# The low half of the attention key, stacked twice: a two-layer decoder trunk on one core

## The chip, the core and the metric

The program runs on one core of one Trainium2 chip. The core has a matrix engine (TensorE, "PE" in the profile, with its weight loads shown apart as "PEld"), a vector engine (VectorE, DVE), an activation engine (ScalarE, ACT), GpSimd (POOL) and a queue engine that issues the DMAs (SyncE, SP). They run side by side and wait for each other by semaphores. TensorE's clock has two levels, 1.2 and 2.4 GHz; the profile gives the granted clock as a share of the full one (0.50 and 1.00). The metric is the device time of the whole program in microseconds; lower is better.

## The reference

The input is one sequence of 1024 positions by 1024 channels in float32. Layer 0 projects it to queries (8 heads of 64), one key and one value of 64 that all heads share, an indexer, and two gating halves. Attention takes for every query the 256 best causal keys by the indexer's score:

```
score = where(causal, einsum(w_idx, relu(qi @ ki.T)), -inf)
idx   = top_k(score, 256)
att   = (q . k[idx]) * 64 ** -0.5          # 8 heads, shared k
out   = softmax(att) @ v[idx]
```

q and k are RMS-normed and rotated. The gating branch and attention are concatenated and projected, and the input is added. An MLP (hidden 4096, squared ReLU), a Conformer convolution module (width 31) and a second MLP follow, each with a residual.

## The kernel before

Every float32 product that matters is made from rounded parts ("fp32r"). A value x is split into hi, which is x rounded to fp32r, and lo = x - hi. The large products add hi*hi, hi*lo and lo*hi (L450 to L452, `products`), each with 128 contraction rows.

In attention the head size is only 64, so the parts are stacked along the contraction rows instead. `q_stack` holds a query head's [hi, lo]; transposed, `q_t` has q_hi in rows 0 to 63 and q_lo in rows 64 to 127. `k_t` holds k_hi twice, in rows 0 to 63 and 64 to 127. One product of 128 rows, L594, so gives (q_hi + q_lo) * k_hi. A second product of 64 rows, L595, adds q_hi * k_lo: it takes rows 0 to 63 of `q_t` and `k_lo_t`, which has 64 rows. Both accumulate in the same PSUM bank:

```
nc.tensor.matmul(dst, q_t[t % 2][:, h, :], k_t[:, c0:c1], start=True, stop=False)
mm = nc.tensor.matmul(dst, q_t[t % 2][0:HD, h, :], k_lo_t[:, c0:c1], start=False, stop=t >= 2)
```

Here HD is 64, P is 128, and t is the query tile of 128 positions, h the head. Tile t sees 128(t+1) keys, in pieces of up to 512 columns and at least 256, so that a head has one pair of products in tiles 0 to 3 and two pairs in tiles 4 to 7. That makes 96 products on either line. In tiles 0 and 1 a product with the triangle (L598) adds the causal mask.

The keys are made during the projections, one tile of 128 positions at a time (`process_keys`, VectorE): after norm and rotation, `k_stack[:, 0:2]` gets k twice, rounded, and `k_stack[:, 2]` gets k minus the rounded part (L1340). `turn_keys` (TensorE, L476 by way of `transpose_group`) transposes the first two, then the third (to 64 rows of PSUM), then the indexer's key. `keys_out` (ScalarE, L969 to L971) copies the results to `k_t`, `k_lo_t` and `ki_t`.

Attention runs in two halves, `attention(0)` for query tiles 0 to 3 and `attention(1)` for tiles 4 to 7; between them lie the first output projection and the MLP of the first half, beside which VectorE does the top-k of tiles 4 to 7. Within a half, heads are numbered a = 8t + h, and the order on TensorE is written out in the loop over a: scores(a), turn_probs(a-2), values(a-3). `scores` waits until VectorE has masked head a-2, whose two PSUM banks it takes over. VectorE adds the mask of the chosen keys and takes the row's maximum (L1490; in tiles 0 and 1 L1494, without top-k) and negates it (L1496). ScalarE takes the exponential (L1066). TensorE transposes the probabilities (L476), ScalarE copies them to `pt_buf` (L1024), and TensorE multiplies them with the values (L617). On ScalarE the order is exp(a), then the copies of head a-2. Three PSUM banks are used in turn for all transposes. In head 4 of a tile the finished rows of the tile before are transposed too (`cat`), which ScalarE (L1031) and VectorE (L1459) split into `hid_buf`; in head 6 the next tile's queries are. In the first half VectorE also does rounds of top-k for tiles 2 and 3 (L1384, L1389) between the heads.

Everything else streams weight tiles through TensorE: 24 products of 512 columns per unit (8 column tiles of 3), with ScalarE (L909) and GpSimd (L733) splitting the next weights.

Of the kernel before, what the change touches and what calls it, by code (L numbers as in the profile page):

```python
# [22 lines left out]
ALU = mybir.AluOpType  # L23
ACT = mybir.ActivationFunctionType
F32 = mybir.dt.float32
F32R = mybir.dt.float32r
# [3 lines left out]
P = 128  # L30
SEQ = 1024
# [4 lines left out]
HEADS, HD = 8, 64  # L36
# [135 lines left out]
def build(nc, x_t, positions, inv_freq, weights, gains, g_head, g_vb, w_s, b_s, w_dw, out_t):  # L172
    with ExitStack() as ctx:
# [3 lines left out]
        def put(name, at, shape, dt=F32):  # L177

            size = int(np.prod(shape[1:])) * 4
            return nc.alloc_sbuf_tensor_at(name, shape, dt, offset=base + at), at + size  # L180
# [10 lines left out]
        zt, a = put("zt", 104 * KB, [P, 3, C0])  # L191
        qz, a = put("qz", a, [P, HALF])
        tmp, a = put("tmp", a, [P, 2, HALF])
        pool_tmp, a = put("pool_tmp", a, [P, HALF])
        junk, a = put("junk", a, [P, HD + ID])
        k_stack, a = put("k_stack", a, [P, 3, HD], F32R)
        ki_stack, a = put("ki_stack", a, [P, 3, ID], F32R)
        assert a <= 120 * KB

# [3 lines left out]
        s_buf, a = put("s_buf", 0, [P, 2, SEQ])  # L203
        p_buf, a = put("p_buf", a, [P, 2, SEQ])
        pt_buf, a = put("pt_buf", a, [P, 2, SEQ])
        q_t0, a = put("q_t0", a, [P, HEADS, P], F32R)
        q_stack, a = put("q_stack", a, [P, HEADS, 2, HD], F32R)
        assert a <= 32 * KB
        k_t, a = put("k_t", 136 * KB, [P, SEQ], F32R)
        k_lo_t, a = put("k_lo_t", a, [HD, SEQ], F32R)  # L210
        v_tok, a = put("v_tok", a, [P, 8, HD])
        score = [None, None]
        for t in range(2, 8):
            s, a = put(f"score{t}", a, [P, P * (t + 1)])
# [8 lines left out]
        ident, a = put("ident", a, [P, P])  # L223
# [223 lines left out]
        def _(pe):  # L447
# [53 lines left out]
            def turn_keys(t):  # L501
                pe.wait_ge(z_proc, 16 * (t // 4) + t % 4 + 1)
                transpose_group(("k", t, 0), lambda bank: [
                    (bank[:, 0:P], k_stack[:, 0:2, :].bitcast(F32).rearrange("p a d -> p (a d)")),
                    (bank[0:HD, P:2 * P], k_stack[:, 2, :].bitcast(F32)),
                    (bank[0:3 * ID, 2 * P:3 * P], ki_stack[:].bitcast(F32).rearrange("p a d -> p (a d)"))])

            def turn_index_queries(t):
# [54 lines left out]
            def attention(half):  # L563
                if half:
                    pe.wait_ge(unit_read, FIRST["wout", 1])

                def cat(t):

                    for g, src in ((0, b_tok[:, t, :]), (1, a_tok[:])):
                        if g:  # L570
                            pe.wait_ge(att_norm, t + 1)
                        transpose_group(("cat", t, g), lambda bank: [
                            (bank[:, i * P:(i + 1) * P], src[:, i * P:(i + 1) * P]) for i in range(4)])

                def queries(t):
                    pe.wait_ge(q_split, t + 1)
                    for g in range(2):
                        transpose_group(("q", t, g), lambda bank: [
                            (bank[:, i * P:(i + 1) * P],
                             q_stack[:, 4 * g + i].bitcast(F32).rearrange("p a d -> p (a d)")) for i in range(4)])  # L580

                def scores(a):

                    t, h = a // 8, a % 8
                    if h == 0:
                        pe.wait_ge(tr_read, TR["q", t, 1] + 1)
                    if a >= 2:
                        pe.wait_ge(qk_masked, a - 1)
                    if 2 <= a < 18:
                        pe.wait_ge(exp_up, a - 1)  # L590
                    for c0 in range(0, P * (t + 1), HALF):
                        c1 = max(min(c0 + HALF, P * (t + 1)), c0 + 2 * P)
                        dst = psum[:, 2 * (a % 2) + c0 // HALF, 0:c1 - c0]
                        nc.tensor.matmul(dst, q_t[t % 2][:, h, :], k_t[:, c0:c1], start=True, stop=False)  # L594
                        mm = nc.tensor.matmul(dst, q_t[t % 2][0:HD, h, :], k_lo_t[:, c0:c1], start=False, stop=t >= 2)  # L595
                    if t < 2:

                        mm = nc.tensor.matmul(dst[:, t * P:(t + 1) * P], ident[:], tri[:], start=False, stop=True)  # L598
                    mm.then_inc(qk_up, 1)

                def turn_probs(a):
                    t = a // 8
                    pe.wait_ge(exp_up, a + 1)
                    for g in range((t + 4) // 4):
                        transpose_group(("p", a, g), lambda bank: [
                            (bank[:, (b % 4) * P:(b % 4 + 1) * P], p_buf[:, a % 2, b * P:(b + 1) * P])
                            for b in range(4 * g, min(4 * g + 4, t + 1))])

                def values(a):
                    t, h = a // 8, a % 8  # L610
                    pe.wait_ge(tr_read, TR["p", a, (t + 4) // 4 - 1] + 1)
                    if h == 0 and t % 4:
                        pe.wait_ge(att_norm, t)
                    if a == 0:
                        pe.wait_ge(spat_used, 8)
                    for b in range(t + 1):
                        mm = nc.tensor.matmul(psum[:, 7, h * HD:(h + 1) * HD], pt_buf[:, a % 2, b * P:(b + 1) * P],  # L617
                                              v_tok[:, b, :], start=(b == 0), stop=(b == t))
                    mm.then_inc(pv_up, 1)

                first, end = 32 * half, 32 * half + 32
                queries(4 * half)
                if half == 0:
                    spatial(7)
                for a in range(first, end + 3):
                    if a < end:
                        if a % 8 == CAT_AT and a // 8 % 4:
                            cat(a // 8 - 1)
                        if a % 8 == Q_AT and a // 8 % 4 < 3:
                            queries(a // 8 + 1)  # L630
                        scores(a)
                    if first + 2 <= a < end + 2:
                        turn_probs(a - 2)
                    if a >= first + 3:
                        values(a - 3)
                cat(4 * half + 3)
# [249 lines left out]
        def _(act):  # L886
# [79 lines left out]
            def keys_out(t):  # L966
                act.wait_ge(tr_up, TR["k", t, 0] + 1)
                bank, cols = psum[:, 4 + TR["k", t, 0] % 3, :], slice(t * P, (t + 1) * P)
                nc.scalar.copy(k_t[:, cols], bank[:, 0:P])  # L969
                nc.scalar.copy(k_lo_t[:, cols], bank[0:HD, P:2 * P])  # L970
                nc.scalar.copy(ki_t[0:3 * ID, cols], bank[0:3 * ID, 2 * P:3 * P]).then_inc(tr_read, 1)  # L971

            def index_queries_out(t):
# [237 lines left out]
        def _(dve):  # L1211
# [110 lines left out]
            def process_keys(s, t):  # L1322
                dve.wait_ge(z_read, s + 1)
                if t >= 1:
                    dve.wait_ge(tr_up, TR["k", t - 1, 0] + 1)
                z = zt[:, t % 3]
                V.tensor_scalar(w_idx[t % 4], z[:, WI0:WI0 + IH], IDX_SCALE, None, ALU.mult)
                V.tensor_scalar(st_v[:, 0:1], st_k[:, t % 2, 0:1], 1.0 / HD, EPS, ALU.mult, ALU.add)
                link(V.tensor_scalar(st_v[:, 1:2], st_k[:, t % 2, 1:2], 1.0 / ID, EPS, ALU.mult, ALU.add))
                rsqrt(r_inv[:, 0:2], st_v[:, 0:2], 2)  # L1330
                kn, kin = z[:, K0:K0 + HD], z[:, KI0:KI0 + ID]
                V.scalar_tensor_tensor(out=kn, in0=kn, scalar=r_inv[:, 0:1], in1=gh[:, 1, :],
                                       op0=ALU.mult, op1=ALU.mult)
                link(V.scalar_tensor_tensor(out=kin, in0=kin, scalar=r_inv[:, 1:2], in1=gh[:, 2, 0:ID],
                                            op0=ALU.mult, op1=ALU.mult))
                kr, kir = tmp[:, 0, 0:HD], tmp[:, 0, HD:HD + ID]
                rope_pair(kr, kn, kir, kin, t)
                V.tensor_copy(k_stack[:, 0:2, :], kr[:, None, :].broadcast_to([P, 2, HD]))
                link(V.tensor_copy(ki_stack[:, 0:2, :], kir[:, None, :].broadcast_to([P, 2, ID])))
                V.tensor_tensor(k_stack[:, 2, :], kr, k_stack[:, 0, :].bitcast(F32), ALU.subtract)  # L1340
                V.tensor_tensor(ki_stack[:, 2, :], kir, ki_stack[:, 0, :].bitcast(F32), ALU.subtract
                                ).then_inc(z_proc, 1)

# [390 lines left out]
```

## Time and profile before

| | us |
|---|---|
| median of 3 runs | 2379.61 |
| lowest and highest | 2375.83, 2385.45 |
| the profiled execution | 2373.25 |
| its span | 2371.5 |
| TensorE busy | 2240.0 |
| VectorE busy | 1378.0 |
| GpSimd busy | 1146.9 |
| ScalarE busy | 848.8 |

Times in the rows are microseconds from the start of the span; in groups by line the mean of one instruction is in nanoseconds. "128\*128" ahead of a product's shape is the stationary tile, rows by columns. TensorE's instructions overlap: a product's row is longer than the distance to the next start, since it includes the way through the array, and weight loads lie beside products. So the busy time of TensorE says little of how fast it works, and the distance from one start to the next is what a product costs. Idle time before an instruction stands in square brackets, with what ended it; "issue" there means that nothing in the profile was waited for.

### The profile page before, as it was taken

The numbers are of one execution on the slowest core, as the hardware profiler recorded it, in microseconds if no ns is written. First come the engines' busy times: TensorE is split into PE (matmuls) and PEld (weight loads), VectorE is DVE, ScalarE is ACT, GpSimd is POOL, SyncE is SP. The second block draws the span as 40 slices with busy tenths as digits, with TensorE's granted clock in tenths as the row PEclk, the third lists the DMA queues.
The fourth block names the chain that finished last, engine by engine and source line by source line (L and its number), as shares of the span: only waits on it lengthen the run. The fifth ranks groups of instructions, "written<-read, shape, count | busy, mean of one in ns | idle before, by whom it ended". The sixth has DMA issues, their size and how long they took to land.

```text
span 2371.5 us, 31721 instructions
## 1 busy us (share of the span) xinstructions
PE 2240.0 (94%) x10040; PEld 1836.8 (77%) x10040; DVE 1378.0 (58%) x2542; ACT 848.8 (36%) x1290; POOL 1146.9 (48%) x642
## 2 busy tenths in 40 slices
PE   4786698999999999999999999999999999999999
PEld 3575576788888877788888888878888887888887
DVE  7888889368888853263777752436777644211111
ACT  4433444432332334434422324363233244322321
POOL 3554522155554600045655645575565565655653
PEclk8888897899999988999999999999999999999999
DMA  5111101123333301023223233223332324333332
GB/s 178 54 54 62 41 5 63 36 89 98 101 94 98 98 18 45 10 86 101 89 98 100 96 98 98 89 90 97 98 98 94 95 88 140 97 93 99 97 97 90
DMA packets 58548, 199.96 MB, mean 84 GB/s; under 512 B 6704, under 2 KB 6960, under 8 KB 58416
## 3 DMA queue, kind: packets, MB, share of 16 engines
q1 hardware_dynamic: 58416, 198.22, 26.5%
q8 instruction: 81, 1.33, 0.2%
q14 instruction: 51, 0.42, 0.1%
HBM read 194.00 MB, written 4.19 MB: 84 GB/s over the span
## 4 chain that ended last, share of the span: by engine, by line
PE 81%; DVE 6%; issue 3%; ACT 1%; POOL 1%; DVEq 0%; ACTq 0%; POOLq 0%
PE psum L450 24%; PE psum L451 24%; PE psum L452 24%; PE psum L617 3%; PE psum L476 2%; PE psum L595 2%; PE psum L594 1%; DVE score L1389 1%; DVE small L1384 1%; DVE small L1232 0%; PE psum L533 0%; DVE small L1231 0%; DVE small L1230 0%; POOL w_buf L733 0%; DVE score L1374 0%
## 5 line engine op out<-in xcount | busy, mean ns | idle before, releaser
L733 POOL TENSOR_TENSOR w_buf<-raw,w_buf 128x1024 fp32r<-128x1024 f32 x336 | 814.8, 2426 | 784.2 <-ACT w_buf L909 784.0
L450 PE MATMUL psum<-hid_buf,w_buf 128*128 128x512 f32 x1344 | 526.0, 391 | 4.6 <-DVE hid_buf L1459 2.8
L909 ACT ACTIVATE w_buf<-raw 128x1024 fp32r<-128x1024 f32 x336 | 353.2, 1052 | 493.9 <-PE psum L452 484.5
L452 PE MATMUL psum<-hid_buf,w_buf 128*128 128x512 f32 x1344 | 523.8, 390 | 0.0
L451 PE MATMUL psum<-hid_buf,w_buf 128*128 128x512 f32 x1344 | 523.6, 390 | 0.0
L450 PE MATMUL psum<-h_buf,w_buf 128*128 128x512 f32 x1216 | 475.3, 391 | 1.4 <-POOL h_buf L841 1.4
L452 PE MATMUL psum<-h_buf,w_buf 128*128 128x512 f32 x1216 | 473.3, 389 | 0.0
L451 PE MATMUL psum<-h_buf,w_buf 128*128 128x512 f32 x1216 | 473.2, 389 | 0.0
L1534 DVE TENSOR_TENSOR xt<-xt,psum 128x512 f32 (+1 forms) x160 | 110.0, 688 | 356.6 <-PE psum L452 356.2
L1555 DVE SCALAR_TENSOR_TENSOR psum<-y_buf,wdw,psum 128x512 f32<-128x512 f32 x464 | 314.0, 748 | 0.0
L450 PEld LDWEIGHTS psum<-hid_buf,w_buf 128*128 128x128 f32 x1344 | 252.7, 188 | 58.6 <-DVE hid_buf L1459 3.3
L451 PEld LDWEIGHTS psum<-hid_buf,w_buf 128*128 128x128 f32 x1344 | 252.8, 188 | 53.1 <-issue 1.0
L452 PEld LDWEIGHTS psum<-hid_buf,w_buf 128*128 128x128 f32 x1344 | 252.6, 188 | 52.8
L450 PEld LDWEIGHTS psum<-h_buf,w_buf 128*128 128x128 f32 x1216 | 228.3, 188 | 50.0 <-POOL h_buf L841 1.8
L451 PEld LDWEIGHTS psum<-h_buf,w_buf 128*128 128x128 f32 x1216 | 228.3, 188 | 47.9 <-issue 1.0
L452 PEld LDWEIGHTS psum<-h_buf,w_buf 128*128 128x128 f32 x1216 | 228.2, 188 | 47.7
L1596 DVE SCALAR_TENSOR_TENSOR t_ring<-psum,rms_bc 128x512 f32<-128x512 f32 x128 | 88.3, 690 | 256.1 <-PE psum L452 255.4
L1153 ACT ACTIVATE s_ring<-t_ring 128x512 f32<-128x512 f32 x128 | 80.9, 632 | 409.6 <-DVE t_ring L1596 409.6
L1384 DVE MAX8 small<-score 128x8 f32<-128x640 f32 (+3 forms) x192 | 163.1, 883 | 6.7 <-ACT b_tok L956 6.4
L1389 DVE MATCH_REPLACE8 score<-small,score 128x640 f32<-128x640 f32 (+3 forms) x192 | 166.9, 876 | 0.0
L827 POOL TENSOR_TENSOR hid_buf<-s_ring,hid_buf 128x512 f32 x64 | 83.2, 1300 | 134.4 <-ACT hid_buf L1155 134.4
L827 POOL TENSOR_TENSOR h_buf<-s_ring,h_buf 128x512 f32 x64 | 83.1, 1298 | 129.8 <-ACT h_buf L1155 129.5
(194 smaller groups left out, 2338.0 us busy)
## 6 DMA issues: line engine op xcount, KB each, us to landing
raw<-weights SPq DMA_DIRECT2D x352, 512.0 KB, 3.5
xt<-x_t SPq DMA_DIRECT2D x2, 2048.0 KB, 7.9
x_in<-x_t SPq DMA_DIRECT2D x12, 256.0 KB, 4.9
out_t<-xt SPq DMA_DIRECT2D x1, 2048.0 KB, 10.2
out_t<-xt SPq DMA_DIRECT2D x8, 256.0 KB, 2.1
b_tok<-x_t SPq DMA_DIRECT2D x4, 256.0 KB, 5.8
ws<-w_s SPq DMA_DIRECT2D x1, 512.0 KB, 4.3
gvb<-g_vb SPq DMA_DIRECT2D x1, 256.0 KB, 4.2
```

Source lines behind the costliest of these rows:

```text
L450: nc.tensor.matmul(acc, lhs_hi, rhs_hi, start=first, stop=False)
L451: nc.tensor.matmul(acc, lhs_hi, rhs_lo, start=False, stop=False)
L452: return nc.tensor.matmul(acc, lhs_lo, rhs_hi, start=False, stop=last)
L733: nc.gpsimd.tensor_tensor(dst_lo, raw[:, raw_slot], dst_hi.bitcast(F32), ALU.subtract).then_inc(lo_up, 1)
L827: nc.gpsimd.tensor_tensor(flat(hidden, 1, k), s_ring[:, r % 2], flat(hidden, 0, k).bitcast(F32), ALU.subtract).then_inc(hid_lo, 1)
L909: nc.scalar.activation(dst, raw[:, raw_slot], ACT.Copy).then_inc(hi_up, 1)
L1153: nc.scalar.activation(s_ring[:, r % 2], t_ring[:, r % 2], ACT.Square).then_inc(squared, 1)
L1384: V.max(top8[z], score[tiles[z]][:]).then_inc(topk_step, 1)
L1389: V.match_replace(out=s, in_to_replace=top8[z], in_values=s, imm_value=TAKEN).then_inc(topk_step, 1)
L1534: V.tensor_tensor(x, x, psum[:, r, :], ALU.add).then_inc(unit_read, 1)
L1555: ins = V.scalar_tensor_tensor(out=c_buf[:, ct, :] if k == CONV - 1 else acc, in0=yflat(ct, k), scalar=wdw[:, ct, k:k + 1], in1=acc, op0=A ...
L1596: V.scalar_tensor_tensor(out=t_ring[:, r % 2], in0=psum[:, r, :], scalar=0.0, in1=rms_bc[:], op0=ALU.max, op1=ALU.mult).then_inc(unit_read, 1)
```

## The change

The low part of the key is made twice, side by side, is transposed to 128 rows and copied as 128 rows, and the second score product takes all 128 rows of `q_t`. It then adds (q_hi + q_lo) * k_lo where it added q_hi * k_lo before. `k_lo_t` lay in 64 partitions and now lies in 128 at the same address; of the other buffers only `ki_stack` moves, by the 256 bytes a partition that `k_stack` grows. The number of instructions and their order on every engine stay as they are.

```diff
-        k_stack, a = put("k_stack", a, [P, 3, HD], F32R)
+        k_stack, a = put("k_stack", a, [P, 4, HD], F32R)
...
-        k_lo_t, a = put("k_lo_t", a, [HD, SEQ], F32R)
+        k_lo_t, a = put("k_lo_t", a, [P, SEQ], F32R)
...
-                    (bank[0:HD, P:2 * P], k_stack[:, 2, :].bitcast(F32)),
+                    (bank[:, P:2 * P], k_stack[:, 2:4, :].bitcast(F32).rearrange("p a d -> p (a d)")),
...
-                        mm = nc.tensor.matmul(dst, q_t[t % 2][0:HD, h, :], k_lo_t[:, c0:c1], start=False, stop=t >= 2)
+                        mm = nc.tensor.matmul(dst, q_t[t % 2][:, h, :], k_lo_t[:, c0:c1], start=False, stop=t >= 2)
...
-                nc.scalar.copy(k_lo_t[:, cols], bank[0:HD, P:2 * P])
+                nc.scalar.copy(k_lo_t[:, cols], bank[:, P:2 * P])
...
-                V.tensor_tensor(k_stack[:, 2, :], kr, k_stack[:, 0, :].bitcast(F32), ALU.subtract)
+                V.tensor_tensor(k_stack[:, 2:4, :], kr[:, None, :].broadcast_to([P, 2, HD]),
+                                k_stack[:, 0:2, :].bitcast(F32), ALU.subtract)
```

## Rows read from the trace of the kernel before

**Rows 1.** The page, busy time of every engine and its share of the span.

```profile
PE 2240.0 (94%) x10040; PEld 1836.8 (77%) x10040; DVE 1378.0 (58%) x2542; ACT 848.8 (36%) x1290; POOL 1146.9 (48%) x642
```

**Rows 2.** Windows: length, busy time (count) of PE, PEld, DVE, ACT, POOL; clock, DMA, GB/s.

```profile
373.00:392.00 19.00, 17.15 (x84) 13.98 (x84) 16.70 (x49) 8.11 (x28) 6.85 (x9) 0.73 0.38 138
...
420.00:433.00 13.00, 13.00 (x49) 10.16 (x49) 3.82 (x12) 4.92 (x11) 0.00 (x0) 0.50 0.00 1
...
850.00:869.00 19.00, 19.00 (x71) 15.03 (x69) 4.68 (x14) 6.96 (x19) 0.00 (x0) 0.50 0.00 0
...
904.00:930.00 26.00, 24.32 (x152) 18.36 (x152) 11.66 (x28) 12.46 (x27) 0.00 (x0) 1.00 0.14 46
...
970.00:980.00 10.00, 9.58 (x49) 7.86 (x49) 2.26 (x5) 4.39 (x8) 0.00 (x0) 0.66 0.01 1
```

**Rows 3.** Timeline of TensorE, MLP: start, length, engine, line, operation, operands, shape.

```profile
820.27 0.39 PE L451 MATMUL psum<-hid_buf,w_buf 128*128 128x512 f32 x1
820.49 0.39 PE L452 MATMUL psum<-hid_buf,w_buf 128*128 128x512 f32 x1
```

**Rows 4.** Timeline of TensorE, tile 7, a head and the next one's start.

```profile
979.99 0.47 PE L594 MATMUL psum<-k_t,q_t 128*128 128x512 f32 x1
980.39 0.49 PE L595 MATMUL psum<-k_lo_t,q_t 64*128 64x512 f32 x1
...
981.25 0.49 PE L595 MATMUL psum<-k_lo_t,q_t 64*128 64x512 f32 x1
981.67 1.10 PE L476 MATMUL psum<-ident,p_buf 128*128 128x128 f32 x8
...
984.31 0.48 PE L594 MATMUL psum<-k_t,q_t 128*128 128x512 f32 x1
```

**Rows 5.** Timeline of TensorE, tile 5, first score product and first transpose.

```profile
881.70 0.48 PE L594 MATMUL psum<-k_t,q_t 128*128 128x512 f32 x1
...
883.16 0.88 PE L476 MATMUL psum<-ident,p_buf 128*128 128x128 f32 x6
```

**Rows 6.** Timeline of TensorE, tile 4, a head at the low clock.

```profile
856.13 0.78 PE L594 MATMUL psum<-k_t,q_t 128*128 128x512 f32 x1
856.83 0.79 PE L595 MATMUL psum<-k_lo_t,q_t 64*128 64x512 f32 x1
...
858.58 1.33 PE L476 MATMUL psum<-ident,p_buf 128*128 128x128 f32 x5
```

**Rows 7.** Timeline of TensorE, projections at the low clock.

```profile
53.05 0.56 PE L451 MATMUL psum<-hid_buf,h_buf 128*128 128x424 f32 x1
53.41 0.56 PE L452 MATMUL psum<-hid_buf,h_buf 128*128 128x424 f32 x1
```

**Rows 8.** Timeline of TensorE, an index product and what follows.

```profile
340.12 0.39 PE L521 MATMUL psum<-ki_t,qi_t 96*128 96x512 f32 x1
340.35 1.89 PE L533 MATMUL psum<-qz,ws 128*128 128x64 f32 x16
```

**Rows 9.** Timeline of VectorE, first mask of the second half.

```profile
847.18 0.82 DVE L1490 CUSTOM_DVE_ANT_0 s_buf<-psum,score 128x640 f32<-128x640 f32 x1
```

**Rows 10.** VectorE's and ScalarE's timelines for that head of tile 7; groups at 640 columns.

```profile
981.78 1.23 DVE L1490 CUSTOM_DVE_ANT_0 s_buf<-psum,score 128x1024 f32<-128x1024 f32 x1 [4.54 <-PE psum L595]
...
983.23 1.15 ACT L1066 ACTIVATE p_buf<-s_buf,small 128x1024 f32<-128x1024 f32 x1 [3.26 <-DVE small L1496]
...
984.38 1.05 ACT L1024 COPY pt_buf<-psum 128x512 f32<-128x512 f32 x2
...
L1066 ACT ACTIVATE p_buf<-s_buf,small 128x640 f32<-128x640 f32 x8 | 6.6, 828 | 18.0 <-PE psum L476 10.7 <-DVE small L1496 7.2
...
L1490 DVE CUSTOM_DVE_ANT_0 s_buf<-psum,score 128x640 f32<-128x640 f32 x8 | 6.6, 824 | 18.7 <-PE psum L595 18.6
```

**Rows 11.** Timeline of TensorE, the wait behind a concatenation (tile 5, head 4).

```profile
893.12 0.41 PE L476 MATMUL psum<-ident,p_buf 128*128 128x128 f32 x2 [1.35 <-DVE hid_buf L1459]
```

**Rows 12.** Instructions of line 1340: count, shortest, median and longest in ns.

```profile
L1340 DVE TENSOR_TENSOR k_stack<-tmp,k_stack x8: 224/226/2375, 51.6 to 229.5; 128x64 fp32r<-128x64 f32 x8
```

## The prediction, made before the changed kernel ran

> **What bounds the kernel now.** I read the profile in this order: the busy shares, the table of windows, then the timeline of TensorE with VectorE's and ScalarE's beside it. TensorE is busy 94% of the span [rows 1] and, outside the projections and the first third of attention, almost without a pause; what shortens a TensorE-bound stretch shortens the end. The change touches attention (about 344 to 448 us for the first half of the queries, 843 to 990 us for the second) and, slightly, the projections. In the windows, 420 to 433 and 850 to 869 show TensorE busy from end to end with its clock at 0.50, which is 1.2 GHz; 904 to 930 shows it at 1.00, which is 2.4 GHz, and busy 24.3 of 26 us. In 373 to 392 it is VectorE that is busy 16.7 of 19 us [rows 2].
>
> A busy row hides what matters here, so starts have to be compared. In the MLP, one 128-row product of 512 columns starts 0.227 us after another; the weight load lies under the product before it [rows 3]. In a head of query tile 7 (four score products of 512 columns) starts lie 0.40, 0.43, 0.43 and 0.42 us apart, 1.68 in all [rows 4]: nearly twice as much. All four use fp32r operands and accumulate as the MLP's do; what differs is that L594 works on 128 rows and L595 on 64 (the 64*128 in its row). With 256 columns in the second part, two products of 512 and two of 256 take 1.46 [rows 5]. At the low clock that pair of pairs takes 2.45 us, 0.70 from one 512 start to the next [rows 6], while products of 424 columns without a change of rows follow at 0.36 there [rows 7]. The number of rows alone isn't it: a 96-row index product is followed 0.23 us later by one of 128 rows [rows 8]. So each passage from 128 to 64 rows and back costs some 0.2 us (0.3 at the low clock), in which the next weight load doesn't lie under the running product. There are 96 low products, each entered and left once.
>
> The trace shows the spacing and not its cause. The Trainium skill has one (TensorEngine Tiling, Tiling Modes, Key Properties): changing the tiling mode drains TensorE, and 64 rows with 128 columns are in its list of modes, while 96 rows are in none. By it every passage goes with the change, and the sum stands as below; another of its pages says the opposite (under the rivals).
>
> **The change, part by part.** (1) *Score products.* L595 works on 128 rows: same columns, same weights to load as L594, no passage. I price a 512-column product at 0.227 (0.43 at the low clock, from 0.36 for 424 columns), one of 384 at 0.17, one of 256 at 0.12 (0.22), the last two by columns from the 0.227. Bounds of this price: the spacing as now (nothing gained), and the MLP's 0.227; I take the latter, since the MLP's products are the nearest rows in type, rows and columns. Per head: tiles 4 and 5 go from 1.46 to 0.69, tile 6 from 1.58 to 0.80, tile 7 from 1.68 to 0.91, each about 0.77 less; at the low clock 2.45 to 1.30, 1.15 less.
>
> *Second half, 32 heads.* Heads 0 and 1 gain nothing: TensorE has their scores done before VectorE, busy with top-k until then, begins its first mask at 847.18 [rows 9]. Of the other 30, six run wholly at the low clock (6 x 1.15 = 6.9), three begin in it (some 0.95 each, 2.8), and 21 run at the high one (21 x 0.77 = 16.2): 25.9 us. Is TensorE still last then? The chain that could replace it goes from the start of a head's last score product (981.25) by the mask on VectorE (981.78) and the exponential on ScalarE (983.23) to the copies of the transposed probabilities of two heads before (984.38, 1.05 long) [rows 4, 10]. That is 4.2 us; then come 16 value products (1.73) and the scores of the next head but one (0.68 to the start of their last): 6.6 us for two heads, 3.3 each. TensorE itself needs 4.32 now [rows 4], 3.55 after. For tile 4 the mask and the exponential are 0.41 and 0.32 shorter (the groups at 640 columns beside the head above) [rows 10], and the mask starts some 0.1 sooner behind a product of 256 columns. With copies of 0.73, ten value products of 0.104 and scores that take 0.58 to the start of their last, two heads come to 4.7, which is 2.35 each; TensorE's own work there (scores 0.69, five transposes 0.6, values 1.04) is 2.33. So TensorE stays the bound, in tile 4 by nothing. At the three places where the concatenated output is transposed, TensorE waits 1.35 us for VectorE's low part [rows 11]; that chain begins with the scores before it and so moves with them, but a copy in front of the second group of transposes is not moved by the last passage saved: 3 x 0.2 lost. Second half: -25.3 us.
>
> *First half, 32 heads.* In 344 to 392 us VectorE has top-k beside the heads and sets their pace [rows 2]; for the small idle times that it has left I count 1.0 us for heads 0 to 15 and 0.5 for 16 to 21 (bounds: nothing, and the 3.3 us that it idles between 373 and 392 plus as much again behind). Then TensorE is alone and at the low clock until 433: seven heads with one pair of products each, half of the 1.15 above, so 4.0. The last three are at the high clock, where a pair is worth 0.38; the chain as above, with the durations of 512 columns, has room for about 0.22 of it (bounds 0 and 0.38): 0.7, and 0.3 on the tail behind the last scores. Sum: -6.5 us.
>
> (2) *The keys.* L1340 writes 128 columns for 64, eight times at 0.23 us [rows 12]. The extra lies between nothing and as much again (1.8 in all); I take 0.5. The eight transposes load 128 columns of weights for 64, and ScalarE copies 128 partitions for 64: by the neighbours' rows below 0.1 us each. TensorE waits for this step, so I count it on the path: +0.8 us.
>
> *Sum.* 2373.25 (the profiled execution) - 25.3 - 6.5 + 0.8 = 2342.2. The median of the runs shown, 2379.61, lies 6.4 above the profiled time; so the forecast is 2379.6 - 31.0 = **2348.6 us**, 1.3% faster.
>
> **The rivals.** *No gain: rows don't matter.* The gaps could come from something the change keeps, say the short accumulation of two products with one stationary tile. Against it: the MLP's L450 and L451 also load the same tile twice and show no gap. It would give 2379.6 + 0.8 = 2380.4; chance 7%. A section of the Trainium skill would have it so (TensorE: Matmul & The Clock Gate, LDWEIGHTS): a load's time goes by its columns, and 32 rows take as long as 128, so that more rows neither cost nor save. The products' rows at 512 columns agree in length, 0.47 and 0.49 [rows 4]; but a length doesn't say what lies under it.
>
> *Part of the gain: another chain takes over.* If each head of the second half meets a VectorE-ScalarE chain some 0.4 longer than counted, half of the 25.3 is left: 2348.6 + 12.7 = 2361.3; chance 8%. For it: the tie in tile 4. Against: the 0.25 us of slack in tile 7.
>
> *More: the clock.* Some 50 us of the second half run at 1.2 GHz, in four stretches of which 850 to 869 is the longest and 970 to 980 the last and shortest [rows 2]. Three follow waits as in [rows 11], one follows the start. With the passages gone the array has fewer holes, and it might be granted 2.4 GHz sooner. If the low stretches vanished, after the change some 44 us would become 24: 2348.6 - 20 = 2328.6. Half of that is about 2338. Chance 9% for more than 10 us.
>
> *Slower: the clock the other way.* The same waits could bring the clock down for good, if the faster heads make TensorE wait a little in each for ScalarE. Some 55 us that would be at 2.4 GHz would then take nearly as much again: 2348.6 + 50 = 2399. It decides against the old kernel from about 31 us of such time on, that is when over half of the second half's fast heads are slow. Against it: in 904 to 930 the clock stays at 1.00 though TensorE idles 1.7 us of it in small pieces [rows 2]. Chance 4%.
>
> The main case keeps 72%, with its own range of 2338 to 2358 (the sizes of the passages, +-3; the clock's stretches, +-6; the scatter of medians). To leave out no more than 2 in 10 the range is 2330 to 2364. A measurement of this kernel tells about 0.5%, or 12 us, from no change. Faster by more than that: the main case, the clock's gain and three quarters of the partial case, 0.87. Within: 0.09. Slower: 0.04.
>
> **What the profile after would show.** Right: L595 as 128*128; in a fast head of tile 7 starts 0.22 to 0.24 apart within the scores and 3.5 to 3.6 us from head to head; TensorE's idle time on ScalarE's copies (L1024) little above now; the second half of attention some 25 us shorter, everything behind it moved and otherwise the same. Wrong: starts still 0.4 apart (rows don't matter); starts 0.23 apart but new waits for L1066 or L1024 in every head (another chain); the granted clock of 843 to 990 us below or above 0.8 (the clock). The keys are right if their step grows by no more than 0.1 to 0.2 us each.

## The result, and the profile after

| | us |
|---|---|
| median before (4 runs, now with one beside the changed kernel) | 2379.32 |
| median after (4 runs, 2324.85 to 2328.79) | 2325.87 |
| ratio after to before, 95% interval | 0.9774, 0.9755 to 0.9793 |
| profiled execution before, after | 2373.25, 2325.89 |
| its span before, after | 2371.5, 2324.2 |

The change makes the kernel 2.3% faster, by 53 us in the medians and 47 in the two profiled executions. The forecast was 31, and 2325.87 lies 4 us below the stated range. (The kernel before scatters by its clock, as the experiments show, so some of the difference between 53 and 47 is which execution was profiled.) In the experiments an execution over 1.5% above the fastest of its kernel counts as slow; the ratios leave such executions out, and the medians are those of all.

The page of the changed kernel, busy times; VectorE, ScalarE and GpSimd do as much as before, only TensorE is busy for less [rows 1]:

```profile
PE 2180.9 (94%) x10040; PEld 1812.3 (78%) x10040; DVE 1377.8 (59%) x2542; ACT 848.5 (37%) x1290; POOL 1147.2 (49%) x642
```

Where the 47 us went is seen by cutting the span at fixed events: the first score product of each half of attention, and the first product of the output projection behind it (from the timelines). The stretch before attention, 351.3 and 351.8 us, the one between the halves, 396.6 and 396.6, and the rest behind attention, 1372.4 and 1372.5, are the same within 0.5 us. The first half went from 96.8 to 86.8 us, the second from 154.3 to 116.5.

Windows over the two halves, first of the kernel before, then of the changed one; the columns are length, busy time (count) of TensorE, its weight loads, VectorE, ScalarE and GpSimd, then granted clock, share of the DMA engines and GB/s:

```profile
344.00:448.10 104.10, 90.34 (x416) 70.60 (x416) 71.96 (x211) 43.85 (x117) 13.53 (x11) 0.69 0.11 36
843.00:998.50 155.50, 148.23 (x816) 114.92 (x816) 54.54 (x128) 69.20 (x144) 0.00 (x0) 0.85 0.05 18
```
```profile
344.00:438.50 94.50, 72.41 (x416) 62.80 (x416) 71.90 (x212) 43.83 (x119) 13.58 (x11) 0.77 0.12 40
834.00:951.00 117.00, 106.22 (x813) 97.78 (x811) 53.86 (x128) 68.84 (x144) 0.00 (x0) 0.99 0.07 24
```

The clock is the reading that the forecast hadn't. In the second half it is granted at 0.85 before and 0.99 after; 0.85 of 155.5 us means some 47 us at 1.2 GHz, and 0.99 means 3. In the first half it rose from 0.69 to 0.77, some 20 us less at 1.2 GHz.

The passages went as forecast. TensorE's timeline after, a head of tile 7 (start, length, engine, line, operation, operands, stationary tile, shape), to be read beside [rows 4]:

```profile
930.28 0.48 PE L594 MATMUL psum<-k_t,q_t 128*128 128x512 f32 x1
930.60 0.39 PE L595 MATMUL psum<-k_lo_t,q_t 128*128 128x512 f32 x1
930.84 0.40 PE L594 MATMUL psum<-k_t,q_t 128*128 128x512 f32 x1
931.07 0.40 PE L595 MATMUL psum<-k_lo_t,q_t 128*128 128x512 f32 x1
931.31 1.04 PE L476 MATMUL psum<-ident,p_buf 128*128 128x128 f32 x8
932.18 1.90 PE L617 MATMUL psum<-v_tok,pt_buf 128*128 128x64 f32 x16
933.88 0.48 PE L594 MATMUL psum<-k_t,q_t 128*128 128x512 f32 x1
```

Starts are now 0.32, 0.24, 0.23 and 0.24 apart, and a head takes 3.60 us where it took 4.32. The 0.32 behind the first product was priced at 0.227. TensorE's own waits, as the list of waits over the second half gives them (who waited for whom, total, times, longest), are small; the one for copies was feared as the next bound, and it is 1.3 us in all:

```profile
PE psum L476 <- DVE hid_buf L1460: 4.9, 3, 1.8
...
PE psum L594 <- DVE small L1491: 1.6, 1, 1.6
...
PE psum L476 <- ACT pt_buf L1024: 1.3, 4, 0.4
```

In the first half the wait for copies grew:

```profile
PE psum L617 <- ACT pt_buf L1024: 11.5, 13, 1.9
```

It was 5.4 us before (the same list). From the first scores of tile 2 on, where VectorE no longer sets the pace throughout, it is 5.2 us for 1.9 (the timelines' idle times, added up). The keys' subtraction takes 0.29 us for 0.23 [rows 12], eight times, and the stretch before attention is 0.5 us longer:

```profile
L1340 DVE TENSOR_TENSOR k_stack<-tmp,k_stack x8: 291/293/2446, 51.8 to 230.0; 128x128 fp32r<-128x128 f32 x8
```

### The profile page after: what moved, and what is told of

It is laid out like the page before. It is cut to its first block, busy times and chain, and to the rows that moved or that the text cites. A ratio compares the mean times of both kernels' runs of the same rounds, so it can differ in the third digit from the quotient of the medians.

```text
span 2324.2 us, 31721 instructions
## 1 busy us (share of the span) xinstructions
PE 2180.9 (94%) x10040; PEld 1812.3 (78%) x10040; DVE 1377.8 (59%) x2542; ACT 848.5 (37%) x1290; POOL 1147.2 (49%) x642
## 4 chain that ended last, share of the span: by engine, by line
PE 80%; DVE 7%; issue 3%; ACT 2%; POOL 1%; DVEq 0%; ACTq 0%; POOLq 0%
PE psum L450 25%; PE psum L451 25%; PE psum L452 25%; PE psum L617 2%; PE psum L476 1%; DVE score L1390 1%; DVE small L1385 1%; PE psum L594 1%; DVE s_buf L1491 1%; PE psum L595 1%; PE psum L533 0%; DVE small L1232 0%; POOL w_buf L733 0%; DVE small L1231 0%; DVE small L1230 0%
```

## The experiments

The theory after the result: a passage between 128 and 64 rows costs 0.2 us by itself, and the passages, as holes in the array's work, also brought the clock down. The rivals: 64-row products are slow, or lower the clock, by themselves, whatever stands beside them; or the clock fell by the waits and by the pace of the heads, and the faster heads only met it otherwise. Each experiment was timed beside the kernel before on the same chip; that kernel had medians of 2380.35 (first four) and 2380.86 us (last four), each of 19 executions that reach from 2368 and 2374 to 2420 and 2421 us.

### The keys alone

```diff
-                        mm = nc.tensor.matmul(dst, q_t[t % 2][:, h, :], k_lo_t[:, c0:c1], start=False, stop=t >= 2)
+                        mm = nc.tensor.matmul(dst, q_t[t % 2][0:HD, h, :], k_lo_t[0:HD, c0:c1], start=False, stop=t >= 2)
```

(against the changed kernel)

> The keys' low part is stacked twice as in the changed kernel, but the second score product still takes rows 0 to 63. Theory (the gain is all in the score products, the keys cost 0.8 us at most): 2379 to 2381 us, the second half of attention as before, 154 us from its first score product to the first output-projection product. Rival (something of the gain lies in the keys, their transposes or where k_lo_t lies): below 2370 us.

Measured: 2381.62 us (2368.76 to 2436.74), ratio to before 1.0007 (0.9973 to 1.0041). The whole gain is in the second score product, and the longer keys cost nothing that this measurement can tell. Its profile has the passages back, as idle time of the weight loads in front of line 595 (total and times); the kernel before has 21.3 us there, the changed kernel none:

```profile
  issue: 22.1, 79
```

The second half took 163 us in its profiled execution, not 154, with a granted clock of 0.79. So the length of the stretches at 1.2 GHz differs between executions of the same work, which the next experiments have to allow for:

```profile
846.00:1009.00 163.00, 156.24 (x808) 121.93 (x808) 53.04 (x127) 68.69 (x143) 0.00 (x0) 0.79 0.05 17
```

### Ninety-six rows

```diff
-                        mm = nc.tensor.matmul(dst, q_t[t % 2][:, h, :], k_lo_t[:, c0:c1], start=False, stop=t >= 2)
+                        mm = nc.tensor.matmul(dst, q_t[t % 2][0:96, h, :], k_lo_t[0:96, c0:c1], start=False, stop=t >= 2)
```

> The second score product takes 96 rows instead of 128 (it then adds q_lo*k_lo for half of the head's columns only, so the scores differ in their last digits). Theory (what costs is the passage between 128 and 64 rows, not a number of rows below 128): as the changed kernel, 2324 to 2329 us, low products starting 0.23 us apart. Rival 1 (every change of the number of rows costs): as before, 2379 us. Rival 2 (what gains is that more rows are active, which holds the clock up): the passages gone, but low-clock stretches in part back, 2335 to 2350 us.

Measured: 2330.02 us (2328.07 to 2332.96), 1 us above the range expected; ratio 0.9806 (0.9772 to 0.9841), whose interval overlaps that of the change. TensorE's timeline, a head of tile 5:

```profile
880.38 0.48 PE L594 MATMUL psum<-k_t,q_t 128*128 128x512 f32 x1
880.69 0.40 PE L595 MATMUL psum<-k_lo_t,q_t 96*128 96x512 f32 x1
880.93 0.28 PE L594 MATMUL psum<-k_t,q_t 128*128 128x256 f32 x1
881.05 0.28 PE L595 MATMUL psum<-k_lo_t,q_t 96*128 96x256 f32 x1
881.17 0.82 PE L476 MATMUL psum<-ident,p_buf 128*128 128x128 f32 x6
```

96 beside 128 rows costs nothing: 0.12 us from the 96-row product of 256 columns to the transposes, where the 64-row one had 0.31. Not every change of the row count costs, so rival 1 falls, and with it the thought that this was about the number of rows that work. The granted clock of the second half was 0.96 (0.99 in the changed kernel), so rival 2 (more rows hold the clock up) has at most the 3 us between the two profiled second halves for it (119.9 and 116.5), and the medians are no further apart than 4 us.

### The products grouped by rows

```diff
-                    for c0 in range(0, P * (t + 1), HALF):
-                        ...
-                        nc.tensor.matmul(dst, q_t[t % 2][:, h, :], k_t[:, c0:c1], start=True, stop=False)
-                        mm = nc.tensor.matmul(dst, q_t[t % 2][0:HD, h, :], k_lo_t[:, c0:c1], start=False, stop=t >= 2)
+                    for low in range(2):
+                        for c0 in range(0, P * (t + 1), HALF):
+                            ...
+                            if low:
+                                mm = nc.tensor.matmul(dst, q_t[t % 2][0:HD, h, :], k_lo_t[:, c0:c1], start=False, stop=t >= 2)
+                            else:
+                                nc.tensor.matmul(dst, q_t[t % 2][:, h, :], k_t[:, c0:c1], start=True, stop=False)
```

(against the kernel before)

> The kernel before with the products of a head in another order: first the 128-row products of both pieces, then the 64-row ones. In query tiles 4 to 7 a head then has two passages for four, in tiles 0 to 3 nothing changes. Theory (each passage costs 0.2 us, 0.3 at the low clock, whatever stands between): 30 heads x 2 x 0.2 to 0.3 = 13 us saved, and between nothing and 20 us from the clock: 2346 to 2366 us; within a head two starts about 0.23 apart where the row count stays, and 0.4 where it changes. Rival (a 64-row product is itself slow, wherever it stands): 2379 us, starts of 64-row products 0.4 apart among themselves too.

Measured: 2368.89 us (2357.26 to 2503.52), ratio 0.9961 (0.9923 to 0.9998). The longest execution had a clock of 0.843 over the whole span, which makes some 785 us at 1.2 GHz, more than attention is long; what happened in it is open. TensorE's timeline, a head of tile 5 (two products in each of the first two rows, 512 and 256 columns):

```profile
904.92 0.59 PE L598 MATMUL psum<-k_t,q_t 128*128 128x512 f32 x2
905.44 0.62 PE L596 MATMUL psum<-k_lo_t,q_t 64*128 64x512 f32 x2
905.99 0.88 PE L476 MATMUL psum<-ident,p_buf 128*128 128x128 f32 x6
```

In the kernel before, the four score products of such a head took 1.46 us [rows 5]; here they take 1.07, with two passages for four, so 0.2 for each saved. The pair of 64-row products takes 0.55, passage included. With 0.31 for a 64-row product of 256 columns and its passage, as before, 0.24 is left for the one of 512 columns: that of a full product. A 64-row product is not slow by itself, and the rival falls. What it does to the clock is another question.

The median sits 3 us above the expected range, and the profiled execution took 2392.43 us with the second half at a clock of 0.66, worse than the kernel before:

```profile
847.00:1020.00 173.00, 166.06 (x809) 136.86 (x810) 53.68 (x128) 69.10 (x144) 0.00 (x0) 0.66 0.05 16
```

The fastest executions, 2357 to 2359 us with 0.96 over the whole span, lie some 10 us below the fastest of the kernel before (2367.93, 0.96). So at an equal clock the saved passages are worth about 10 of the 13 us expected, but in half of the executions the clock was 0.952 or less and gave some of it back, or more. Fewer passages didn't mean a better clock here, against the theory; why is open.

### The change, padded to the old pace

```diff
+                        for _ in range(2):
+                            nc.tensor.matmul(dst, q_t[t % 2][:, h, :], k_t[:, c0:c1], start=True, stop=True)
                         nc.tensor.matmul(dst, q_t[t % 2][:, h, :], k_t[:, c0:c1], start=True, stop=False)
```

(in the changed kernel; the first two results are overwritten)

> The changed kernel with the first product of every piece made three times, so that a head costs TensorE about as long as before the change (0.23 us for each extra product of 512 columns: 0.69 to 0.91 a head in tiles 4 to 7, 0.24 to 0.45 in tiles 0 to 3), without any passage. Theory (the passages, as holes in the array's work, brought the clock down): the clock stays at 0.97 or more in the second half of attention, which takes 116.5 + 30 x 0.8 = 140 us against 154 before; with the first half some 4 us longer, 2352 to 2356 us. Rival (the clock fell by the waits and by the pace, and the faster heads only met it otherwise): low stretches of some 40 us return in the second half, 154 us or more, 2368 to 2380 us.

Measured: 2350.78 us (2349.27 to 2351.48), 1 us below the range expected, ratio 0.9894 (0.986 to 0.9928). The second half of attention:

```profile
839.00:977.00 138.00, 128.60 (x936) 117.54 (x936) 53.26 (x127) 68.00 (x143) 0.00 (x0) 1.00 0.05 20
```

At the old pace per head and with the same waits for VectorE behind each concatenation, the clock stays at 1.00, and the half takes 138 us for 154. This parts the gain in two. Counted as the ratio counts, the kernel before has a median of 2377.8 us here: 2377.8 - 2350.8 = 27 us come from the clock. The other 2350.78 - 2325.87 = 24.9 us are the price of the padding, which stands for the time of the passages. In the profiled executions the second half gives 16.2 us for the clock (154.3 to 138.1) and 21.6 for the padding (138.1 to 116.5). In the first half, where the padded kernel's clock was higher than the changed one's (0.90 and 0.79 over the half), the parts are 9.1 and 1.0 us and aren't well separated. The rival of waits and pace falls. What isn't tested is a hole of the same length made in another way: no run tells whether the clock goes by the holes themselves or by how dense the work between them is, which the padding raises too.

### Probes of 64 and of 128 rows

```diff
+                        nc.tensor.matmul(dst[:, 0:2 * P], q_t[t % 2][0:HD, h, :], k_lo_t[0:HD, c0:c0 + 2 * P], start=True, stop=True)
                         nc.tensor.matmul(dst, q_t[t % 2][:, h, :], k_t[:, c0:c1], start=True, stop=False)
```

(in the changed kernel; the control has `0:P` for `0:HD`)

> The changed kernel, with one product of 64 rows and 256 columns ahead of each pair of score products; its result is overwritten. Each head gets back as many passages as before the change (two per piece), and all products that count have 128 rows. Theory (passages cost 0.2 us at the high clock and, as holes, bring the clock down): beside the same kernel with 128-row probes, 30 heads x 4 x 0.19 = 23 us more in the second half and 4 in the first, 2362 us, and low-clock stretches of 30 us and more return in the second half, 2375 us or more. Rival (the clock went down because half the array stood still in the 64-row score products): the clock stays at 0.97 or more in the second half, 2355 to 2365 us.

> The same probes with 128 rows: the control for the cost of the extra products. Theory: 0.12 us for each, two a head in the 30 heads of the second half, 7 us, and 1 to 2 in the first half: 2333 to 2336 us, the clock as in the changed kernel. Rival (any third product in the group costs what the 64-row probe costs): the same time as with 64-row probes.

Measured: 2370.47 us with 64-row probes (2359.02 to 2399.03), ratio 0.9954 (0.9909 to 0.9998); 2333.11 us with 128-row probes (2329.95 to 2336.23), ratio 0.9814 (0.9788 to 0.9841). TensorE's timeline with 64-row probes, a head of tile 5, and then the windows of the second half, with 64-row and with 128-row probes (the first window is set in round numbers; with 64-row probes the half runs from 839.5 to 1012.2, and over that stretch the clock is 0.79 too):

```profile
873.64 0.38 PE L594 MATMUL psum<-k_lo_t,q_t 64*128 64x256 f32 x1
873.95 0.49 PE L595 MATMUL psum<-k_t,q_t 128*128 128x512 f32 x1
874.28 0.39 PE L596 MATMUL psum<-k_lo_t,q_t 128*128 128x512 f32 x1
874.60 0.38 PE L594 MATMUL psum<-k_lo_t,q_t 64*128 64x256 f32 x1
```
```profile
836.00:1008.00 172.00, 164.40 (x865) 131.86 (x865) 53.89 (x127) 67.93 (x142) 0.00 (x0) 0.79 0.05 16
```
```profile
835.00:957.00 122.00, 111.21 (x872) 103.52 (x872) 53.46 (x127) 68.22 (x143) 0.00 (x0) 1.00 0.07 23
```

From the probe to its successor it is 0.31 us at 64 rows; in the control 0.11 or 0.12 (0.21 behind the values). Around the probe the starts are 0.1 further apart than in the control as well (0.32 and 0.33 for 0.23), so that the 0.2 is the mean of a passage and not what each single one takes. The four executions with 64-row probes whose clock was 0.972 to 0.974 over the span took 2359 to 2361 us; against the control, with 0.973 to 0.975, that is 27 us, which is what 30 heads x 4 x 0.19 and 4 in the first half come to. The others fall to 0.949 and rise to 2399 us. Here all products that count have 128 rows, and the granted clock of the second half in the profiled execution is 0.79 for 1.00. So the clock doesn't need the half-used array of the long products to go down; passages with short 64-row products are enough. The probes are 64-row products too, so what a passage does to the clock isn't parted here from what 64 rows do to it. And they don't always bring it down: four of the ten executions lie within 2361 us. The expected 2375 or more was too sure; the median is 2370.

### The kernel before, padded

The same two extra products, with the 64-row products left.

> The kernel before with its passages, and with the first product of every piece made three times (dense work of 0.69 to 0.91 us a head between the passages). Theory (the clock goes down when too much of the time is holes): the dense work keeps the clock up in most of the second half, which pays for it: 24 us in the second half and 5 in the first added, some 25 taken back, 2380 to 2392 us, and runs scatter less than before's. Rival (passages bring the clock down however much dense work lies between): nothing taken back, and the low stretches stretch with the work, 2409 to 2420 us.

Measured: 2385.5 us (2381.6 to 2421.31), ratio 1.0036 (0.9997 to 1.0074). The second half:

```profile
840.00:1010.00 170.00, 162.95 (x936) 124.86 (x934) 52.81 (x125) 68.27 (x143) 0.00 (x0) 0.92 0.05 16
```

By the padded change some 25 us of work were added (29 by the estimate), and the time rose by 5. The clock of the second half is 0.92 (27 us at 1.2 GHz, for 47 before), and of the window of the first half 0.83, for 0.69. So the same passages bring the clock down less when there is more dense work between them. The rival (nothing taken back) falls. Runs still scatter as before's do, against what was expected.

Beside the padded change, whose second half takes 138 us with the same extra products, this is the pure effect of 64 against 128 rows: 2385.5 - 2350.8 = 34.7 us (on two chips, on which the kernel before differs by 0.5).

### More passages on the same columns

```diff
+                        for b0 in ((c0, c0 + 2 * P) if c1 - c0 == HALF else (c0,)):
+                            b1 = b0 + 2 * P if c1 - c0 == HALF else c1
+                            part = dst[:, b0 - c0:b1 - c0]
+                            nc.tensor.matmul(part, q_t[t % 2][:, h, :], k_t[:, b0:b1], start=True, stop=False)
+                            mm = nc.tensor.matmul(part, q_t[t % 2][0:HD, h, :], k_lo_t[:, b0:b1], start=False, stop=t >= 2)
```

(in the kernel before, for its two products)

> The kernel before with each piece of 512 columns cut into two of 256, high and low product in turn: two more passages for each such piece, 80 in the second half and 16 in tile 3, on the same columns. Theory: 96 x 0.2 to 0.3 = 19 to 29 us for the passages, 2400 to 2408 us at the clock as before, and more where the low stretches grow, up to 2440 us. Rival (the cost goes with the columns of 64-row products, not with the passages): no change beyond 5 us, 2380 to 2385 us.

Measured: 2471.35 us (2465.86 to 2476.85), ratio 1.0384 (1.0347 to 1.042): 90 us slower, where 20 to 60 were expected. The second half, and TensorE's timeline in it:

```profile
859.00:1104.00 245.00, 240.38 (x888) 191.85 (x887) 52.78 (x125) 68.81 (x143) 0.00 (x0) 0.53 0.03 11
```
```profile
879.99 0.56 PE L597 MATMUL psum<-k_t,q_t 128*128 128x256 f32 x1
880.48 0.58 PE L598 MATMUL psum<-k_lo_t,q_t 64*128 64x256 f32 x1
880.99 0.58 PE L597 MATMUL psum<-k_t,q_t 128*128 128x256 f32 x1
```

A clock of 0.53 means that nearly the whole half ran at 1.2 GHz. The cost goes with the number of passages and not with the columns, and 96 more of them were enough to hold the clock down throughout; in the kernel before it rose again between 904 and 930 [rows 2], and here not. (This run too has the same 64-row columns as the kernel before, so the columns alone don't set the clock.)

## Why the prediction was wrong

**What bounds.** Right: TensorE bounds attention but for the heads with top-k, and what was saved there arrived at the end without loss (1372.4 and 1372.5 us behind attention).

**The passages.** Right in their time, and by now measured three ways: the changed kernel's timeline, the grouped products (0.2 for each saved), and the probes (27 us for 27 expected at equal clock). The padded change's 24.9 us are the price of products of about that length and not of the passages themselves. A head of tile 7 went from 4.32 to 3.60 us, 0.72 for 0.77 forecast, and one of tile 4 at the high clock from 3.10 to 2.4. The term's small error is the first product of a head: its successor comes after 0.32, not 0.227 us.

**The rule weighed.** The Trainium skill (TensorEngine Tiling, Tiling Modes, Key Properties) has a drain at each change of the tiling mode, with 64 rows in its list and 96 not. The runs agree: 0.31 from a 64-row probe of 256 columns to its successor, 0.12 from one of 128 rows, and 0.12 behind 96 rows. The Trainium skill's rule on load times by columns (TensorE: Matmul & The Clock Gate, LDWEIGHTS) held too, 183 ns at 64 rows and 192 at 128 for the loads of line 595 (medians). It said nothing on the passages: their time was lost ahead of the load and not in it.

**The bound behind it.** Right for the second half: copies held up TensorE for 1.3 us in all, and the waits at the concatenations grew by 0.15 us each (1.35, 1.48 and 1.62 before) for 0.2 forecast. Heads 0 and 1 gained nothing, as forecast; TensorE then waits 1.6 us for their first mask, where it had waited 0.25. In the first half the heads of tiles 0 and 1 gained 1.6 us for 1.0 forecast, and the rest 8.5 for 5.5, although the waits for copies grew there by 3.3 us: the clock's part was larger.

**The keys.** 0.5 us before attention for 0.8 forecast, and within the noise alone.

**The clock: the step that failed.** Between forecast and median lie 22.7 us. Of these 16.4 are in the profiled executions (47.4 us gained for 31.0), 12.5 of them in the second half (37.8 for 25.3) and 3.5 in the first (10.0 for 6.5). The other 6.4 are the step from the profiled time to the median, which the forecast carried over from the kernel before; the changed kernel's median is its profiled time. Both parts come from taking the clock, and its scatter, as they were. In the sum, six heads of the second half ran wholly at 1.2 GHz and three began in it, seven more stood in the first, and all were taken to be at 1.2 GHz still after the change ("six run wholly at the low clock (6 x 1.15 = 6.9), three begin in it"). The text gave the clock's stretches +-6 us, and a gain of over 10 us by them a chance of 9%, and put it at 20 us at the most. In fact the stretches went with the passages: in the profiled executions some 47 us at the low clock in the second half became 3, and some 64 in the first became 43. By the padded change the clock was worth some 27 us, as much as the passages' own time. The rival had the mechanism ("with the passages gone the array has fewer holes") and looked at the second half alone; beside it stood only that three of the four stretches follow waits. The waits stayed: 1.50, 1.63 and 1.77 us behind the concatenations, longer than before. The windows of the changed kernel that hold them:

```profile
867.00:876.00 9.00, 7.11 (x56) 6.43 (x55) 3.43 (x8) 5.07 (x12) 0.00 (x0) 1.00 0.01 3
892.00:900.00 8.00, 6.02 (x47) 5.41 (x46) 3.56 (x8) 5.05 (x10) 0.00 (x0) 1.00 0.71 243
924.00:931.00 7.00, 4.98 (x36) 4.39 (x36) 2.58 (x5) 3.96 (x8) 0.00 (x0) 1.00 0.00 0
```

These waits alone didn't bring the clock down. The trace before had a hint of it: from 850 to 869 TensorE was busy without a pause by its rows and stayed at 0.50 [rows 2], so the passages were the holes that were left to ask about. The sign that the prediction named for this case, a granted clock of 843 to 990 us away from 0.8, came: 0.99. (That kernel before had 0.84 there, so the sign as written was a loose one.) And one reading, against the rival of a clock that falls for good, was wrong: the 1.7 us that TensorE idles between 904 and 930 us aren't small pieces, since 1.48 of them are the wait for the second concatenation, which ends at 929.98, right ahead of the third low stretch.

**What stays open.** The clock isn't a function of the number of holes alone. Grouping the products halved them in the second half and the clock of its profiled execution was lower, 0.66; the same kernel with 64-row probes gave 2359 and 2399 us. The runs show the direction (no passages: 1.00 or 0.99 in the second halves of the three kernels with 128 rows throughout, 0.96 with 96 rows; passages: 0.53 to 0.92), and not the rule by which a single stretch begins or ends. Every run with passages also has 64-row products, so that for the clock, other than for the time, the two aren't parted. And passages aren't the only thing that lowers it: in the first half of the changed kernel, which has none and where TensorE often waits, the clock is still 0.77.

## What to carry to other kernels

Read the distance between starts, not busy time, where products with different row counts alternate; if it exceeds that of equal neighbours, stacking or duplicating an operand up to 128 rows can be free, and here it gave 0.2 us per passage. The products' rows don't show these holes as idle; the weight loads' do (21.3 us in front of line 595 before, none after). With them went most of the time at the lower clock in the second half, so where a stretch is at 1.2 GHz although its engine looks busy, a change that closes such holes should be priced a second time with the stretch at 2.4 GHz, and that case given a chance of its own size.

## What the runs showed of the hardware

- Passages between 64 and 128 rows cost some 0.2 us at 2.4 GHz (starts 0.43 us apart for 0.23 at 512 columns) and 0.3 at 1.2 GHz (0.70 us apart for 0.42, the changed kernel's at 418.03) each; between 96 and 128 rows there is nothing to be seen (0.12 us between starts at 256 columns).
- 96 more passages took the second half's granted clock from 0.85 to 0.53 and cost 90 us in all, three to nearly five times their own length (19 to 29 us).
- Behind the fp32 value products, and behind the fp32 transposes (0.32 at 866.97 in the changed kernel), the first fp32r score product is followed after 0.32 us instead of 0.23, at 512 columns, with 128 rows on both sides. No run tells whether that is the type or the change of operands.
- Waits of 1.50 to 1.77 us for another engine left the clock at 1.00 in the second half of the changed kernel, where the work between them was dense; in the kernel before, with passages, low stretches followed waits of 1.35 to 1.62 us.
